# Combining a differential head's two probability maps before the transposes, and norming from the accumulators

## The chip, the cores and the metric

One core of a Trainium2 chip runs the whole program. The time is the device time of one execution in microseconds; the number quoted for a kernel is the median of its runs. The profiled execution is one further run, and its trace gives a span, from the first to the last instruction, and a start time for every instruction.

## What is computed

The program is two small transformer stacks run one after the other on 256 tokens of width 1024: four blocks (feed-forward, mixer, feed-forward) and then two larger layers. Every matrix is fp32. The mixer changes with the block. Block 2, and only block 2, uses the differential mixer, `mixer_c` of the reference:

```
q = q.reshape(B, nb, Q_BLOCK, HEADS_C, 2, HEAD_DIM_C).transpose(1, 0, 2, 3, 4, 5)    # 8 heads, 2 maps, 64
k = k.reshape(B, S, HEADS_C, 2, HEAD_DIM_C)
v = v.reshape(B, S, HEADS_C, 2 * HEAD_DIM_C)                                          # 128 wide, one for both maps
lam_full = jnp.exp(jnp.sum(lamf[0] * lamf[1])) - jnp.exp(jnp.sum(lamf[2] * lamf[3])) + lambda_init
...
    s = jnp.einsum('bqhmd,bkhmd->bmhqk', qblk, k).astype(jnp.float32) * scale + alibi
    s = jnp.where(allowed, s, NEG_INF)
    p = jax.nn.softmax(s, axis=-1)
    a = p[:, 0] - lam_full * p[:, 1]
    return jnp.einsum('bhqk,bkhe->bqhe', a.astype(v.dtype), v)
...
o = rms_norm(o, subln_g) * (1.0 - lambda_init)
return o.reshape(B, S, D) @ w_o
```

Each of the eight heads has two softmax maps over the same value rows; their difference, the second weighted by `lam_full`, is multiplied with the values, and each head's 128 outputs are normed by their own root mean square.

## The kernel before

The five engines run hand-written instruction streams that meet at semaphores. Outside attention the program is a chain of fp32 weight products on PE. Weights arrive in a ring of 9 slots and are split in two parts, by ACT (`high`) and DVE (`low`), up to three chunks ahead. The same stages run in the same order on each engine.

`units_of` lists what an attention has to do. For the differential mixer a unit is one map of one head for one tile of 128 queries: 16 units for tile t=0, which sees 128 keys, and 16 for tile t=1, which sees 256. `groups_of` joins units into groups: four units (two heads) in t=0, so groups 0 to 3, and two units (one head) in t=1, so groups 4 to 11. Either way a group has 512 score columns. An accumulator `acc` is one PSUM bank for two heads; in t=0 one group fills it, in t=1 two groups do. There are eight of them, named (t, b) here with b = 0 to 3.

All engines run a software pipeline over i, the number of the group, in their own function `attention`:

- PE in step i: scores of group i; transposes of group i-2 (it waits for `weighed`, the exponentials of ACT); the product of group i-3 with the values into the accumulator (it waits for the copy of the transposes out of PSUM). In step 13 the `tail` begins the transposes of the finished tile 0 of `o_rows` for the output product; their fourth pair comes after the loop, and its bank is the one that DVE frees with the first pair of `tile_low`.
- DVE in step i: scale and bias of the scores (L2000), the row maximum (L2002), for t=0 the copy of the transposes of group i-2 (L2010; ACT does it for t=1), and for a finished accumulator `evacuate`, here `f` of `differential`: reciprocal of four sums (L2064), the second map's factor times minus `lam_full` (L2066), the first map scaled (L2069), and the second added, a head at a time (L2071), into `o_rows`. The norm of the accumulator before is woven around it: `mean_of_heads` (L2046) ahead, `normed` (L2055) behind. In step 14 the `tail` is `tile_low`, the low part of the transposed tile 0 (L1941).
- ACT in step i: the sums of squares of a finished pair of heads (`head_squares`, L1432), for t=1 the copy of the transposes of group i-2 (L1295), and the exponentials of group i with their sums (L1457). After the loop come `head_squares` of (1, 2), `tile_high` of tile 0, and `head_squares` of (1, 3).
- POOL raises each mean to the power -0.5 (L1728), between `mean_of_heads` and `normed`.

Accumulators come from three banks in turn (`SUMMED`), score banks from three (`SCORES`), banks for transposes from two (`TB`). After attention PE goes on with the output product of tile 0, waits for tile 1's last norm, and never stops again for long in this block.

## Time and profile before

| | |
|---|---|
| median of 3 runs | 3040.71 us (3039.13 to 3049.1) |
| profiled execution | 3042.0 us, its span 3040.3 us |
| PE busy in the span | 2992.0 us, 98% |
| DVE, ACT, POOL busy | 1850.5, 1480.4, 84.1 us |
| mean granted TensorE clock | 0.999 of full speed |
| differential attention in the trace | from 1232.4 to 1268.4 us |

The trace's start times are counted from the start of the span. A row's duration is that of the instruction; the next instruction of an engine may start before it ends, so the distance between two starts is read beside it. "PE busy" counts pipelined matmuls to their modelled ends.

### The profile page before, as it was taken

To read this page: it belongs to the slowest core of one execution; us is meant where nothing else is said; L and a number is where in the kernel's file an instruction comes from. 1 tells how busy PE (TensorE), PEld (TensorE's weight loads), DVE (VectorE), ACT (ScalarE), POOL (GpSimd) and SP (SyncE) were. 2 spreads that over 40 slices of the span, in tenths; PEclk is the share of its full clock that TensorE was granted. 3 is DMA by queue.
4 is the path that set the end of the run, shared out by engine and by line. 5 is a ranking of instruction groups with operands and counts; after the bars stand their busy time and mean duration, and the time that the engine had idled before them with its cause. 6 is when DMAs were issued, how large, how long until landed. Compare 5 with 4: busy or idle time off the path is not lost.

```text
span 3040.3 us, 38290 instructions
## 1 busy us (share of the span) xinstructions
PE 2992.0 (98%) x15499; PEld 2526.9 (83%) x15499; DVE 1850.5 (61%) x2322; ACT 1480.4 (49%) x2163; POOL 84.1 (3%) x153
## 2 busy tenths in 40 slices
PE   8999999999999999999999999999999999999999
PEld 6889888888888888888888988897888889788887
DVE  5556655546655546755554665469775547977553
ACT  5445544435544435554443564354655434565542
POOL 0000000000000001000000000010000001000000
PEclk9999999999999999999999999999999999999999
DMA  7564455555555555265555635576244548615453
GB/s 229 186 208 141 161 192 177 194 190 199 183 181 190 190 181 186 84 201 188 193 180 175 219 119 193 179 203 210 84 159 150 190 166 226 200 69 171 152 189 126
DMA packets 302403, 532.98 MB, mean 175 GB/s; under 512 B 31074, under 2 KB 125204, under 8 KB 302228
## 3 DMA queue, kind: packets, MB, share of 16 engines
q1 hardware_dynamic: 288964, 511.63, 51.4%
q10 hardware_dynamic: 13264, 18.90, 1.8%
q8 instruction: 124, 2.03, 0.3%
q14 instruction: 51, 0.42, 0.0%
HBM read 528.33 MB, written 1.11 MB: 174 GB/s over the span
## 4 chain that ended last, share of the span: by engine, by line
PE 89%; DVE 8%; ACT 1%; issue 1%; DMA 1%; ACTq 0%; POOL 0%; SPq 0%; POOLq 0%; DVEq 0%
PE bank L724 85%; DVE sb_arena L2280 3%; DVE sb_parts L1819 2%; PE bank L1025 2%; PE bank L1053 1%; PE bank L805 1%; DMA sb_ring<-in_w_xq_dram 1%; ACT sb_parts L1321 0%; DVE sb_sc L2000 0%; PE bank L788 0%; PE bank L780 0%; ACT sb_sc L1457 0%; DVE sb_prT L2010 0%; POOL sb_rstd L1728 0%; DMA sb_ring<-in_ff_w_in_dram 0%
## 5 line engine op out<-in xcount | busy, mean ns | idle before, releaser
L1819 DVE TENSOR_TENSOR sb_parts<-sb_ring,sb_parts 128x2048 fp32r<-128x2048 f32 x480 | 1097.4, 2290 | 788.8 <-ACT sb_parts L1321 786.5
L724 PE MATMUL bank<-sb_parts,sb_hT_high 128*128 128x512 f32 (+1 forms) x4480 | 1370.0, 392 | 7.0 <-DVE sb_parts L1819 6.7
L1321 ACT ACTIVATE sb_parts<-sb_ring 128x2048 fp32r<-128x2048 f32 x480 | 914.5, 1913 | 790.6 <-PE bank L724 695.8
L724 PEld LDWEIGHTS bank<-sb_parts,sb_hT_high 128*128 128x128 f32 x4480 | 835.7, 188 | 184.4 <-DVE sb_parts L1819 11.0
L724 PE MATMUL bank<-sb_parts,sb_hT_low 128*128 128x512 f32 (+1 forms) x2240 | 853.0, 390 | 0.0
L724 PE MATMUL bank<-sb_parts,sb_hidden_high 128*128 128x512 f32 x1760 | 553.7, 395 | 0.0
L724 PEld LDWEIGHTS bank<-sb_parts,sb_hT_low 128*128 128x128 f32 x2240 | 420.9, 188 | 88.0
L724 PEld LDWEIGHTS bank<-sb_parts,sb_hidden_high 128*128 128x128 f32 x1760 | 328.3, 187 | 80.3 <-issue 0.6
L724 PE MATMUL bank<-sb_parts,sb_hidden_low 128*128 128x512 f32 x880 | 347.0, 394 | 0.0
L724 PE MATMUL bank<-sb_hT_high,sb_parts 128*128 128x256 f32 x1408 | 254.5, 283 | 0.0
L724 PEld LDWEIGHTS bank<-sb_hT_high,sb_parts 128*128 128x128 f32 x1408 | 220.1, 192 | 0.2
L724 PE MATMUL bank<-sb_hT_low,sb_parts 128*128 128x256 f32 x704 | 199.2, 283 | 0.0
L724 PEld LDWEIGHTS bank<-sb_parts,sb_hidden_low 128*128 128x128 f32 x880 | 164.7, 187 | 40.7
L724 PE MATMUL bank<-sb_parts,sb_oT_high 128*128 128x512 f32 (+1 forms) x616 | 177.9, 390 | 0.8 <-ACT sb_oT_high L1295 0.8
L1295 ACT ACTIVATE sb_hidden_high<-bank 128x512 fp32r<-128x512 f32 x110 | 60.4, 597 | 210.4 <-PE bank L1025 210.4
L1981 DVE TENSOR_TENSOR sb_hidden_low<-bank,sb_hidden_high 128x512 fp32r<-128x512 f32 x110 | 71.3, 686 | 107.4 <-ACT sb_hidden_high L1295 107.4
L724 PEld LDWEIGHTS bank<-sb_hT_low,sb_parts 128*128 128x128 f32 x704 | 135.1, 192 | 0.2
L724 PEld LDWEIGHTS bank<-sb_parts,sb_oT_high 128*128 128x128 f32 x616 | 112.6, 188 | 24.9 <-issue 3.0
L1457 ACT ACTIVATE sb_sc<-sb_sc,sb_nmax 128x256 f32<-128x256 f32 (+3 forms) x224 | 95.3, 427 | 73.7 <-DVE sb_nmax L2002 73.6
L1728 POOL TENSOR_TENSOR sb_rstd<-sb_mean_sq,sb_minus_half 128x1 f32<-128x1 f32 (+1 forms) x79 | 49.9, 632 | 2895.7 <-DVE sb_mean_sq L1838 2532.0
L1405 ACT ACTIVATE sb_prT<-bank,sb_rstd 128x512 f32<-128x512 f32 x100 | 69.2, 692 | 116.8 <-PE bank L724 116.8
L724 PE MATMUL bank<-sb_parts,sb_oT_low 128*128 128x512 f32 (+1 forms) x308 | 107.2, 386 | 0.0
(220 smaller groups left out, 2083.8 us busy)
## 6 DMA issues: line engine op xcount, KB each, us to landing
sb_ring<-in_ff_w_in_dram SPq DMA_DIRECT2D x160, 1024.0 KB, 5.2
sb_ring<-in_ff_w_out_dram SPq DMA_DIRECT2D x88, 1024.0 KB, 4.9
sb_ring<-in_w_gate_up_dram SPq DMA_DIRECT2D x40, 1024.0 KB, 5.2
sb_ring<-in_w_in_dram SPq DMA_DIRECT2D x38, 1024.0 KB, 5.2
sb_ring<-in_a_w_qkv_dram SPq DMA_DIRECT2D x24, 1024.0 KB, 5.3
sb_ring<-in_w_down_dram SPq DMA_DIRECT2D x22, 1024.0 KB, 5.0
sb_ring<-in_ff_w_in_dram SPq DMA_DIRECT2D x32, 512.0 KB, 4.8
sb_ring<-in_c_w_qkv_dram SPq DMA_DIRECT2D x12, 1024.0 KB, 5.1
```

The lines of the kernel that those rows point to most:

```text
L724: return nc.tensor.matmul(o, lhsT, rhs, start=start, stop=stop)
L805: ins = nc.tensor.transpose(o, i, ident[:, :])
L1025: ins = nc.tensor.transpose(bank[:, c * S + t * P:c * S + (t + 1) * P], hid_f[:, t, (2 * b + c) * P:(2 * b + c + 1) * P], ident[:, :])
L1053: ins = nc.tensor.transpose(bank[0:n, c:c + P], sc[:, (i - 2) % 3, k0:k0 + n], ident[:, :])
L1295: return nc.scalar.activation(o, i, ACT.Copy, scale=scale)
L1321: nc.scalar.activation(halves(n, slice(0, filled(n))).high, ring[:, raw_in[n], 0:filled(n)], ACT.Copy) \
L1405: nc.scalar.activation(silu[:, t, :], G.of((st, "gate", g, t))[:, :], ACT.Silu, scale=row_factor_of(st, t)) \
L1457: ins = nc.scalar.activation(part_of, part_of, ACT.Exp, bias=nmax[:, i % 3, j:j + 1], accum_out=sums[:, u["t"], u["col"]:u["col"] + 1])
L1728: pool.tensor_tensor(rstd[:, c0:c0 + n], mean_sq[:, c0:c0 + n], minus_half[:, 0:n], ALU.pow) \
L1819: V.tensor_tensor(both.low, ring[:, raw_in[n], 0:filled(n)], both.high.bitcast(F32), ALU.subtract) \
L1981: V.tensor_tensor(hidT.low[:, k:k + 2, :], G.of((st, "hid", g, b))[:, :].rearrange("p (c s) -> p c s", c=2), hidT.high[:, k:k + 2, :].bitc ...
L2280: ins = V.scalar_tensor_tensor(convT[:, c, :], src, wt, convT[:, c, :], ALU.mult, ALU.add)
```

## The change

Since both maps of a head meet the same value rows, the difference can be taken between the maps. The exponentials stay unnormalised: with first and second sums s1 and s2 the kernel now forms e1 - lam_full (s1/s2) e2, which is s1 times the wanted map. The factor s1 carries through to the output, and the norm removes it, if its guard EPS is multiplied by s1 squared.

The diff, with lines that are context left out:

```diff
@@ units_of
-                            acc=(st, "o", t, s // per), c0=(s % per) * width, width=width, col=s, head=s))
+                            acc=(st, "o", t, s // per), c0=(s % per if i % 3 == 0 else s // 2 % 2) * width,
+                            width=width, col=s, head=s))
@@ groups_of
+                maps = 2 if kind == "mix" and i % 3 == 2 else 1
-                                   rows=u["blocks"][0][1], blocks=len(u["blocks"]), width=P * n * len(u["blocks"]),
+                                   rows=u["blocks"][0][1], blocks=len(u["blocks"]), width=P * n // maps * len(u["blocks"]),
@@ PE attention
-                        pe.wait_ge(weighed.sem, weighed.at((st, i - 2)))
+                        if g["maps"] == 2:
+                            pe.wait_ge(dve_step.sem, dve_step.at((st, "combined", i - 2)))
+                        else:
+                            pe.wait_ge(weighed.sem, weighed.at((st, i - 2)))
-                        for j, u in enumerate(g["units"]):
+                        for j, u in enumerate(g["units"][::g["maps"]]):
...
@@ ACT head_squares
-                act.wait_ge(dve_read.sem, dve_read.at(acc))
+                act.wait_ge(matmul_done.sem, matmul_done.at((st, "pv", b if t == 0 else 5 + 2 * b)))
-                    ins = nc.scalar.activation(xn[:, 0, 512:640], o_rows[:, t, c:c + P], ACT.Square,
+                    ins = nc.scalar.activation(xn[:, 0, 512:640], G.of(acc)[:, m * P:(m + 1) * P], ACT.Square,
@@ ACT attention
-                    if differential and i >= 5 and groups[i - 5]["last"]:
-                        head_squares(st, groups[i - 5]["acc"])
+                    if differential and i >= 4 and groups[i - 4]["last"]:
+                        head_squares(st, groups[i - 4]["acc"])
@@ DVE
+            def combine(st, i, g):
+                t, c = g["t"], g["units"][0]["col"]
+                ratio = inv[:, t, c + 1:c + g["n"]:2]
+                dve.wait_ge(weighed.sem, weighed.at((st, i)))
+                step(V.reciprocal(ratio, sums[:, t, c + 1:c + g["n"]:2]))
+                step(V.scalar_tensor_tensor(ratio, ratio, lam[:, 6:7], sums[:, t, c:c + g["n"]:2], ALU.mult, ALU.mult))
+                for m in range(0, g["n"], 2):
+                    first, second = (sc[:, i % 3, n * g["kn"]:(n + 1) * g["kn"]] for n in (m, m + 1))
+                    ins = V.scalar_tensor_tensor(first, second, inv[:, t, c + m + 1:c + m + 2], first, ALU.mult, ALU.add)
+                ins.then_inc(dve_step.sem, dve_step.next((st, "combined", i)))
@@ DVE attention
+                    if means:
+                        means()
...
+                    if 1 <= i <= len(groups) and groups[i - 1]["maps"] == 2:
+                        combine(st, i - 1, groups[i - 1])
...
+                    if norms:
+                        norms()
@@ differential: mean_of_heads
+                    step(V.scalar_tensor_tensor(guard, first_sums, EPS / factor ** 2, first_sums, ALU.mult, ALU.mult))
                     dve.wait_ge(squared.sem, squared.at((st, "subln", t, b)))
-                    V.tensor_scalar(mean_sq[:, 8 * t + 2 * b:8 * t + 2 * b + 2], ssum[:, 2 * b:2 * b + 2], 1.0 / (P * factor ** 2),
-                                    EPS / factor ** 2, ALU.mult, ALU.add) \
+                    V.scalar_tensor_tensor(mean_sq[:, 8 * t + 2 * b:8 * t + 2 * b + 2], ssum[:, 2 * b:2 * b + 2],
+                                           1.0 / (P * factor ** 2), guard, ALU.mult, ALU.add) \
@@ differential: normed
-                        o = o_rows[:, t, h * P:(h + 1) * P]
-                        ins = V.scalar_tensor_tensor(o, o, rstd[:, 8 * t + h:8 * t + h + 1], subln[:, :], ALU.mult, ALU.mult)
+                        ins = V.scalar_tensor_tensor(o_rows[:, t, h * P:(h + 1) * P], G.of(acc)[:, m * P:(m + 1) * P],
+                                                     rstd[:, 8 * t + h:8 * t + h + 1], subln[:, :], ALU.mult, ALU.mult)
+                    settle(dve, ins, dve_read, acc)
@@ differential: f
-                    cols = inv[:, t, 4 * b:4 * b + 4]
-                    step(V.reciprocal(cols, sums[:, t, 4 * b:4 * b + 4]))
-                    step(V.tensor_scalar(cols[:, 1:4:2], cols[:, 1:4:2], lam[:, 6:7], None, ALU.mult))
-                    both = bank[:, :].rearrange("p (h m d) -> p h m d", h=2, m=2)
-                    t0 = tmp[:, 0:256].rearrange("p (h d) -> p h d", h=2)
-                    step(V.tensor_tensor(t0, both[:, :, 0, :], spread(cols[:, 0:4:2], P), ALU.mult))
-                    for h in range(2):
-                        ins = V.scalar_tensor_tensor(o_rows[:, t, (2 * b + h) * P:(2 * b + h + 1) * P], both[:, h, 1, :],
-                                                     cols[:, 2 * h + 1:2 * h + 2], t0[:, h, :], ALU.mult, ALU.add)
-                    ins.then_inc(dve_read.sem, dve_read.next(acc))
```

What is left of `f` waits for the accumulator and marks it open; `means` and `norms` of the next step then do its mean and norm. Only the last accumulator is finished at once.

Three places show how the instructions move. On DVE, one step of t=1 that finishes an accumulator, before: mean of the accumulator before, evacuation, norm, and then the scores of the next group (`sb_sc<-bank,sb_arena` is scale and bias, `sb_nmax` the maximum).

```order
L2046 TENSOR_SCALAR sb_mean_sq<-sb_ssum 128x2 [waits squared,matmul_done]
L2064 RECIPROCAL sb_inv<-sb_sums 128x4
L2066 TENSOR_SCALAR sb_inv<-sb_inv,sb_lam 128x2 [waits dve_step]
L2069 TENSOR_TENSOR sb_tmp<-bank,sb_inv 128x256 [waits dve_step]
L2071 SCALAR_TENSOR_TENSOR sb_o_rows<-bank,sb_inv,sb_tmp 128x128 [waits dve_step]
L2071 SCALAR_TENSOR_TENSOR sb_o_rows<-bank,sb_inv,sb_tmp 128x128
L2055 SCALAR_TENSOR_TENSOR sb_o_rows<-sb_o_rows,sb_rstd,sb_subln 128x128 [waits rstd_ready]
L2055 SCALAR_TENSOR_TENSOR sb_o_rows<-sb_o_rows,sb_rstd,sb_subln 128x128
L2000 SCALAR_TENSOR_TENSOR sb_sc<-bank,sb_arena 128x512 [waits transposed,scored]
L2002 TENSOR_REDUCE sb_nmax<-sb_sc 128x2 [waits dve_read]
```

The same place of the changed kernel, one whole step: the guard and the mean come first, then the scores, then the combination of the group before (`sb_sc<-sb_sc,sb_inv`), then the norm, which now reads a bank.

```order
L2069 SCALAR_TENSOR_TENSOR sb_inv<-sb_sums 128x2 [waits matmul_done,dve_read]
L2071 SCALAR_TENSOR_TENSOR sb_mean_sq<-sb_ssum,sb_inv 128x2 [waits squared,dve_step]
L2018 SCALAR_TENSOR_TENSOR sb_sc<-bank,sb_arena 128x512 [waits transposed,scored]
L2020 TENSOR_REDUCE sb_nmax<-sb_sc 128x2 [waits dve_read]
L1994 RECIPROCAL sb_inv<-sb_sums 128x1 [waits weighed]
L1995 SCALAR_TENSOR_TENSOR sb_inv<-sb_inv,sb_lam,sb_sums 128x1 [waits dve_step]
L1998 SCALAR_TENSOR_TENSOR sb_sc<-sb_sc,sb_inv 128x256 [waits dve_step]
L2081 SCALAR_TENSOR_TENSOR sb_o_rows<-bank,sb_rstd,sb_subln 128x128 [waits rstd_ready]
L2081 SCALAR_TENSOR_TENSOR sb_o_rows<-bank,sb_rstd,sb_subln 128x128
```

The five evacuation instructions per accumulator are gone, and three for every group have come. At the end of DVE's loop, before, nothing stood between the norm of the accumulator before and `tile_low` (`sb_oT_low`); in the changed kernel the guard, mean and norm of (1, 2) stand there:

```order
L1994 RECIPROCAL sb_inv<-sb_sums 128x1 [waits weighed]
L1995 SCALAR_TENSOR_TENSOR sb_inv<-sb_inv,sb_lam,sb_sums 128x1 [waits dve_step]
L1998 SCALAR_TENSOR_TENSOR sb_sc<-sb_sc,sb_inv 128x256 [waits dve_step]
L2081 SCALAR_TENSOR_TENSOR sb_o_rows<-bank,sb_rstd,sb_subln 128x128 [waits rstd_ready]
L2081 SCALAR_TENSOR_TENSOR sb_o_rows<-bank,sb_rstd,sb_subln 128x128
L2069 SCALAR_TENSOR_TENSOR sb_inv<-sb_sums 128x2 [waits matmul_done,dve_read]
L2071 SCALAR_TENSOR_TENSOR sb_mean_sq<-sb_ssum,sb_inv 128x2 [waits squared,dve_step]
L2081 SCALAR_TENSOR_TENSOR sb_o_rows<-bank,sb_rstd,sb_subln 128x128 [waits rstd_ready]
L2081 SCALAR_TENSOR_TENSOR sb_o_rows<-bank,sb_rstd,sb_subln 128x128
L1945 TENSOR_TENSOR sb_oT_low<-bank,sb_oT_high 128x128 [waits act_step,dve_read]
```

So two rounds of `normed` now precede `tile_low` where one did. On ACT, the end of the loop of the changed kernel has a pair of squares on either side of the copy of the last group:

```order
L1436 ACTIVATE sb_xn,sb_ssum<-bank 128x128 [waits squared,matmul_done]
L1436 ACTIVATE sb_xn,sb_ssum<-bank 128x128 [waits squared]
L1300 ACTIVATE sb_prT<-bank 128x256 [waits matmul_done,transposed]
L1436 ACTIVATE sb_xn,sb_ssum<-bank 128x128 [waits squared,matmul_done]
L1436 ACTIVATE sb_xn,sb_ssum<-bank 128x128 [waits squared]
L1300 ACTIVATE sb_oT_high<-bank 128x128 [waits transposed]
```

The pair after the copy is the old call behind the loop, `head_squares(st, (st, "o", NT - 1, 2))`, which the diff leaves in place. Step 13 of the loop now squares (1, 2) too, so this accumulator is squared twice, and DVE's mean waits for the second time. POOL's and SP's instructions are the same in both kernels.

## Rows read from the trace of the kernel before

**Rows 1.** The page: busy time of each engine, its share and instructions.
```profile
PE 2992.0 (98%) x15499; PEld 2526.9 (83%) x15499; DVE 1850.5 (61%) x2322; ACT 1480.4 (49%) x2163; POOL 84.1 (3%) x153
```

**Rows 2.** Windows: stretch, length, busy PE, PEld, DVE, ACT, POOL, PEclk, DMA.
```profile
1246.00:1254.00 8.00, 6.46 (x43) 5.69 (x44) 7.62 (x26) 5.38 (x22) 2.10 (x3) 1.00 0.01 3
```

**Rows 3.** The chain that ended last, 1205 to 1290: start, us, what.
```profile
1236.72 0.66 PE bank L1053 x4
...
1267.56 0.50 DVE sb_oT_low L1941 x2
...
1268.60 5.55 PE bank L724 x24
```

**Rows 4.** Timeline of DVE in the attention: start, us, instruction.
```profile
1233.50 0.76 DVE L2000 SCALAR_TENSOR_TENSOR sb_sc<-bank,sb_arena 128x256 f32<-128x256 f32 x2 [0.47 <-PE bank L724]
...
1234.90 0.75 DVE L2000 SCALAR_TENSOR_TENSOR sb_sc<-bank,sb_arena 128x256 f32<-128x256 f32 x2
...
1249.45 0.17 DVE L2064 RECIPROCAL sb_inv<-sb_sums 128x4 f32<-128x4 f32 x1
1249.66 0.23 DVE L2066 TENSOR_SCALAR sb_inv<-sb_inv,sb_lam 128x2 f32<-128x2 f32 x1
...
1250.91 0.61 DVE L2055 SCALAR_TENSOR_TENSOR sb_o_rows<-sb_o_rows,sb_rstd,sb_subln 128x128 f32<-128x128 f32 x2
1251.43 0.69 DVE L2000 SCALAR_TENSOR_TENSOR sb_sc<-bank,sb_arena 128x512 f32<-128x512 f32 x1
...
1252.75 0.16 DVE L2046 TENSOR_SCALAR sb_mean_sq<-sb_ssum 128x2 f32<-128x2 f32 x1
...
1260.81 0.68 DVE L2000 SCALAR_TENSOR_TENSOR sb_sc<-bank,sb_arena 128x512 f32<-128x512 f32 x1
```

**Rows 5.** Groups by form on DVE, 1233 to 1275: count, busy, mean ns.
```profile
L2071 DVE SCALAR_TENSOR_TENSOR sb_o_rows<-bank,sb_inv,sb_tmp 128x128 f32<-128x128 f32 x16 | 4.9, 347 | 0.3
L2055 DVE SCALAR_TENSOR_TENSOR sb_o_rows<-sb_o_rows,sb_rstd,sb_subln 128x128 f32<-128x128 f32 x16 | 4.9, 345 | 0.8 <-POOL sb_rstd L1728 0.8
...
L2000 DVE SCALAR_TENSOR_TENSOR sb_sc<-bank,sb_arena 128x256 f32<-128x256 f32 x8 | 3.0, 418 | 0.5 <-PE bank L724 0.5
...
L2010 DVE COPY sb_prT<-bank 128x512 f32<-128x512 f32 x4 | 2.7, 682 | 0.0
```

**Rows 6.** Single lines elsewhere: duration ns min/median/max, first and last start, forms.
```profile
L1887 DVE SCALAR_TENSOR_TENSOR sb_x<-sb_xn,sb_rstd,sb_x x48: 741/747/753, 203.3 to 1985.0; 128x512 f32<-128x512 f32 x48
...
L2188 DVE COPY sb_arena<-bank x12: 424/425/426, 261.7 to 1740.0; 128x256 f32<-128x256 f32 x12
```

**Rows 7.** Groups by form on ACT, 1233 to 1275.
```profile
L1457 ACT ACTIVATE sb_sc<-sb_sc,sb_nmax 128x256 f32<-128x256 f32 x16 | 8.0, 500 | 3.3 <-DVE sb_nmax L2002 3.3
```

**Rows 8.** Timelines late in the attention: ACT, PE and DVE.
```profile
1266.36 0.31 ACT L1432 ACTIVATE sb_xn<-sb_o_rows 128x128 f32<-128x128 f32 x1 [0.78 <-DVE sb_o_rows L2071]
...
1267.10 1.09 ACT L1295 ACTIVATE sb_oT_high<-bank 128x128 fp32r<-128x128 f32 x6
...
1257.69 0.60 PE L1053 MATMUL bank<-sb_ident,sb_sc 128*128 128x128 f32 x4
...
1259.02 1.03 PE L724 MATMUL bank<-sb_arena 128*128 128x256 f32 x4
1259.89 0.60 PE L1053 MATMUL bank<-sb_ident,sb_sc 128*128 128x128 f32 x4
...
1268.43 1.17 PE L724 MATMUL bank<-sb_parts,sb_oT_high 128*128 128x512 f32 x4
...
1272.03 0.17 DVE L2046 TENSOR_SCALAR sb_mean_sq<-sb_ssum 128x2 f32<-128x2 f32 x1 [0.39 <-ACT sb_xn L1432]
1273.01 0.61 DVE L2055 SCALAR_TENSOR_TENSOR sb_o_rows<-sb_o_rows,sb_rstd,sb_subln 128x128 f32<-128x128 f32 x2 [0.81 <-POOL sb_rstd L1728]
```

**Rows 9.** Windows where the granted clock fell, in a later layer.
```profile
2667.00:2670.00 3.00, 1.51 (x9) 0.95 (x8) 2.54 (x11) 2.21 (x3) 0.00 (x0) 1.00 0.22 33
...
2673.00:2676.00 3.00, 3.00 (x9) 2.35 (x8) 1.13 (x6) 2.97 (x11) 0.00 (x0) 0.50 0.00 0
```

35 lines of the change are left out of this document (21 added, 14 removed).

## Prediction

> **What bounds the kernel now.** I read the page first. PE is busy for 2992.0 of 3040.3 us [rows 1], so a change can only show where PE is not, or where it moves PE's own work. The edit touches one stage of some forty, the differential attention from 1232.4 to 1268.4 us: 36 us in all. Were the whole stage free the kernel would gain 1.2%. A window inside it has PE at 6.46 and DVE at 7.62 of 8 us [rows 2]: here DVE is the tighter engine. The chain that ended last says the same: PE runs it as far as the first transposes of the stage, and it ends in DVE's low part of tile 0, the last pair of transposes and then 5.55 us of output product without a gap [rows 3]. So two numbers decide: when DVE comes to the scores of the last group (group 11, at 1260.81 us [rows 4]), and how long it takes from there until the output product starts (at 1268.43 us [rows 8], 7.62 us later).
>
> DVE's own timeline gives prices as distances between starts. A four-unit step costs 1.40 us for scores and maximum (1233.50 to 1234.90), a two-unit step 1.32 (1251.43 to 1252.75). An evacuation costs 1.46 (1249.45 to 1250.91), a norm 0.52 (1250.91 to 1251.43), a reciprocal that the next instruction waits for 0.21 (1249.45 to 1249.66) [rows 4]. Beside the busy times this yields a rule of thumb: the next instruction starts 0.08 us before the end of one that it doesn't wait for (0.61 against 0.52 for the norm), and 0.04 after the end of one that it does (0.17 against 0.21). With it a copy of 128x512 costs 0.60 and the mean 0.08 [rows 5, 4].
>
> As a check, before: four steps at 1.40, seven at 1.32 (groups 4 to 10), four copies 2.4, five evacuations 7.3, four norms 2.1 and four means 0.3 make 26.9 us. From 1233.50 to 1260.81 are 27.31 us. DVE has nearly no idle time there, so its instructions add up to its time.
>
> **The change part by part.** On PE each group has half its transposes and half its value products. From one group's transposes to the next group's PE takes 2.20 us (1257.69 to 1259.89), 0.87 of it the scores [rows 8]; the other 1.33 halve, which leaves 1.5 us a step. PE only has to stay ahead of DVE, so this is worth nothing on the path: the cover is DVE's work, and PE had 1.5 us of 8 free already [rows 2]. On ACT the copies shrink to 128x256, hidden likewise.
>
> On DVE, removed: five evacuations before 1260.81, 7.3 us, and half of each of four copies. A 128x256 copy is busy for 0.42 us [rows 6], so it costs 0.34 in place of 0.60, four times: 1.0 us. Old mean and norm go too, 2.4 us.
>
> Added, the combination. Reciprocal 0.21; the tiny product with a pointer scalar, nearest row the 0.23 us of L2066 [rows 4], 0.27 with its wait. The large operation reads SBUF twice. For 128x128 its row is 345 ns and its step 0.26; for 128x256 the trace has the same operation from PSUM at 418 ns [rows 5], and from SBUF I interpolate 480 ns between 345 for 128 and 747 for 512 columns [rows 5, 6]. I take a step of 0.40, with bounds 0.34 (418 less 0.08) and 0.60 (had it to be the price of a 512-column maximum). So a four-unit group costs 0.21 + 0.27 + 2 x 0.26 = 1.00 us, a two-unit group 0.88. Groups 0 to 3 and 4 to 9 come before the scores of group 11: 4.0 + 5.3 = 9.3 us.
>
> Added, the mean with guard and the norm that must settle: guard 0.16 + 0.04 = 0.20 (priced as L2046, the same width with a constant [rows 4]), mean 0.08, norm 0.26 + 0.38 = 0.64 since the next instruction waits for the bank's release. That is 0.92 us, and five of them (accumulators of t=0 and the first of t=1) come before: 4.6 us. One new wait: the combination of group 0 needs its exponentials, which end at about 1236.68, when PE's first transposes were released [rows 3]; DVE is there at 1236.30, so 0.4 us, against 0.3 us that DVE waited for scores elsewhere. Later groups have the exponentials in time: two of 500 ns [rows 7] against 1.32 + 0.88 us of DVE work between the maximum and the combination of one group.
>
> Sum to the scores of group 11: +9.3 + 4.6 + 0.1 - 7.3 - 1.0 - 2.4 = +3.3 us, so they start at about T = 1264.1. Bounds: two-unit combinations at 0.67 (reciprocal 0.17, product 0.16, large step 0.34) and four-unit ones at 0.85 take 1.9 us off; at 1.1 us each they add 1.4.
>
> **The end of the stage**, counted from T. The maximum is done at 1.45, exponentials 11 at 2.6, combination 11 at 3.5. PE, after the product of group 9 and the six early transposes of tile 0, does the transposes of group 11 by 4.2. ACT has squared accumulator (1, 2) by then; it copies group 11 by 4.6 and squares (1, 2) a second time, 0.74 us (1266.36 to 1267.10 [rows 8]), until 5.4. DVE's mean waits for this, and the norm starts 0.98 us after the mean, POOL's power lying between (1272.03 to 1273.01 [rows 8]): 6.35. The norm costs 0.64 and only then does the low part of tile 0 start, at 7.0. From there to the output product it was 0.87 us (1267.56 [rows 3] to 1268.43 [rows 8]). Total 7.9 us, where it was 7.62. So the shorter route to the squares is given back by the second squaring and by the round through POOL that now stands in front of the low part. ACT's high part starts at 5.4 and is not what is late. Tile 1's last norm: squares after ACT's high part at about 9.3, norm done by 11.0; PE needs it at 7.9 + 5.55 = 13.4. It is hidden.
>
> Together +3.3 + 0.3 = +3.6 us, bounds +1.5 and +5.5. The stage is followed by PE work without gaps, so the shift reaches the end. The profiled run was 3042.0 us with a span of 3040.3, and the median is 3040.71: I add the shift to the median, 3044.3 us.
>
> **A rule against the trace.** The norm now reads a PSUM bank in place of SBUF. In this trace the two kinds of operand cost the same for 128 columns: 347 and 345 ns [rows 5], so I charge nothing. The Trainium skill, "VectorE: DVE Perf Modes", section "The TRN2 errata", has a fixed cost of 58 cycles for a SBUF source and 120 for PSUM at 0.96 GHz, an estimate of 0.065 us more for each norm instruction. By it the ten before T would add 0.65 us and the sum would be +4.2 instead of +3.6; the measured rows decide.
>
> **The rivals.**
>
> *The change is a gain of DVE work, and the stage shrinks.* For it speaks that the last evacuation chain of 1.46 us leaves the end and that t=0 steps carry less. If DVE were not the bound, its added 9.3 us would vanish in idle time. Against it: the check sum above leaves under 0.5 us idle in 27. If it held, the end would be 1.46 us shorter and the middle the same: 3039.3 us. Chance 0.06.
>
> *The granted clock falls at the end of the stage.* After its last transposes at T+4.2 PE has, until T+7.9, only the products of groups 10 and 11, about 1.1 us. In this kernel one such thin stretch, 1.51 us busy of 3, was followed by a window at 0.50 of the granted clock, 1.2 in place of 2.4 GHz [rows 9]; 1.5 us were lost. Before, with 6.46 of 8 us busy, it stayed at 1.00 [rows 2]. Then the time is 3044.3 + 1.6 = 3045.9 us. Chance 0.35, inside the same band. The Trainium skill, "TensorE: Matmul & The Clock Gate", Part 1, calls the throttled clock the default that activity releases; the trace's one fall is in line with that.
>
> *The clock falls for the whole attention: the other side.* PE's 1.5 us per step become 3.1 at half clock, where DVE now takes 2.7 on average (1.32 + 0.88 + half of 0.92). PE is then the bound in all twelve steps: 12 x 0.4 = 5 us, and 1.6 at the end, on top of 3.6: 3051 us, 0.33% slower. It decides only if the clock is low through nearly all steps. Against it: by these numbers PE still works 1.5 of 2.7 us in the middle, and more by the measure of the windows, which counts matmuls to their ends, no less than in the stretch before the fall. Chance 0.04.
>
> *Nothing moves.* If DVE's instructions had cover that I don't see, or the combination met its lower bound and the second squaring were early, the time is 3041 to 3042. Chance 0.10, and it can't be told from my forecast by the clock on the wall.
>
> The forecast without a clock fall has 0.45.
>
> **How the numbers follow.** A measurement of this kernel can tell about 0.3%, 9.1 us, from no change: that is 3031.6 to 3049.8. The forecast, its bounds of +1.5 to +5.5, the clock's 1.6 us, and the shrinking stage all lie inside it. Only the rival on the other side lies out, and the scatter of the runs shown, where one of three is 8.4 us above the median. So faster 0.01, within 0.3% 0.94, slower 0.05. The range runs from the shrinking stage, 3039.3, to the upper bound with the clock, 3047.8, and 2 us more for the scatter of a median.
>
> **What the profile would show.** Scores of the last group 3.3 us later than before, counted from the scores of the first; DVE busy in the middle with almost no idle time. Combination rows near 0.48 us for 128x256. Nine pairs of squares on ACT, the eighth right before the high part. DVE idle for nearly a microsecond ahead of the norm of (1, 2), waiting for POOL, with the low part behind it; the output product 34.9 + 3.6 us after the first scores. A clock below 1.00 around the end would show the second rival. I am wrong if DVE waits in the middle, for exponentials or for scores behind PE's products; if the large combination costs 0.6 us or more; or if PE's start doesn't hang on the low part of tile 0.

## The result, and the profile after

| | before | changed |
|---|---|---|
| median of 17 runs each | 3040.84 us | 3047.91 us |
| ratio | | 1.0021, interval 1.0014 to 1.0028 |
| profiled execution, its span | 3042.0, 3040.3 us | 3044.74, 3043.0 us |

The change costs 7.1 us by the medians and 6.4 us by the ratio (4.3 to 8.5). The prediction was 3044.3 us, range 3039.3 to 3049.8, with 0.94 on "within 0.3%". The measured median is inside the range and 3.6 us above the point. The stage's trace has a place for 1.6 us of that gap, and the rest stays open. Three runs at 4571.8 us (e4), 5339.5 us (e10) and 13122.9 us (before, beside e9 to e11) are in a slow state and stand in no mean, median or ratio below.

Two distances tell the stage: from the first scores on DVE to the last (group 11), and from the first scores to the output product on PE. Before they were 27.31 and 34.93 us [rows 4, 8]. After they are 30.67 and 38.41. The page of the changed kernel:

```profile
span 3043.0 us, 38167 instructions
...
PE 2986.1 (98%) x15427; PEld 2519.0 (83%) x15427; DVE 1850.1 (61%) x2330; ACT 1477.9 (49%) x2167; POOL 83.5 (3%) x153
```

DVE's total hardly moved (1850.5 before [rows 1]). PE has 72 matmuls less and is not faster for it. The timeline of DVE, changed kernel (start, us, instruction), shows the first scores, the first combination, one whole combination with the norm and the mean behind it, the last scores and the end:

```profile
1232.42 0.76 DVE L2018 SCALAR_TENSOR_TENSOR sb_sc<-bank,sb_arena 128x256 f32<-128x256 f32 x2 [0.47 <-PE bank L726]
...
1235.61 0.17 DVE L1994 RECIPROCAL sb_inv<-sb_sums 128x2 f32<-128x2 f32 x1 [0.33 <-ACT sb_sc L1461]
1235.81 0.22 DVE L1995 SCALAR_TENSOR_TENSOR sb_inv<-sb_inv,sb_lam,sb_sums 128x2 f32<-128x2 f32 x1
1236.07 0.61 DVE L1998 SCALAR_TENSOR_TENSOR sb_sc<-sb_sc,sb_inv 128x128 f32<-128x128 f32 x2
1236.60 0.75 DVE L2018 SCALAR_TENSOR_TENSOR sb_sc<-bank,sb_arena 128x256 f32<-128x256 f32 x2
...
1249.99 0.15 DVE L1994 RECIPROCAL sb_inv<-sb_sums 128x1 f32<-128x1 f32 x1
1250.18 0.22 DVE L1995 SCALAR_TENSOR_TENSOR sb_inv<-sb_inv,sb_lam,sb_sums 128x1 f32<-128x1 f32 x1
1250.43 0.48 DVE L1998 SCALAR_TENSOR_TENSOR sb_sc<-sb_sc,sb_inv 128x256 f32<-128x256 f32 x1
1250.84 0.60 DVE L2081 SCALAR_TENSOR_TENSOR sb_o_rows<-bank,sb_rstd,sb_subln 128x128 f32<-128x128 f32 x2
1251.47 0.16 DVE L2069 SCALAR_TENSOR_TENSOR sb_inv<-sb_sums 128x2 f32<-128x2 f32 x1
1251.67 0.16 DVE L2071 SCALAR_TENSOR_TENSOR sb_mean_sq<-sb_ssum,sb_inv 128x2 f32<-128x2 f32 x1
1251.75 0.69 DVE L2018 SCALAR_TENSOR_TENSOR sb_sc<-bank,sb_arena 128x512 f32<-128x512 f32 x1
...
1263.09 0.69 DVE L2018 SCALAR_TENSOR_TENSOR sb_sc<-bank,sb_arena 128x512 f32<-128x512 f32 x1
...
1268.35 0.16 DVE L2071 SCALAR_TENSOR_TENSOR sb_mean_sq<-sb_ssum,sb_inv 128x2 f32<-128x2 f32 x1 [1.03 <-ACT sb_xn L1436]
1269.32 0.61 DVE L2081 SCALAR_TENSOR_TENSOR sb_o_rows<-bank,sb_rstd,sb_subln 128x128 f32<-128x128 f32 x2 [0.81 <-POOL sb_rstd L1732]
1269.96 1.28 DVE L1945 TENSOR_TENSOR sb_oT_low<-bank,sb_oT_high 128x128 fp32r<-128x128 f32 x6
```

The reader sees the whole price here. A four-unit combination takes 0.99 us (1235.61 to 1236.60), a two-unit one 0.85 (1249.99 to 1250.84), norm, guard and mean together 0.91 (1250.84 to 1251.75). Nothing waits in between, so the new work adds straight to the stage. Up to the last scores the timeline notes only three waits of DVE behind its first instruction: the 0.33 us shown, 0.27 and 0.22. At the end DVE waits twice, for ACT's second squaring (1.03) and for POOL (0.81), before the low part may start at 1269.96.

PE's timeline in the changed kernel has the other half of the story:

```profile
1236.74 0.52 PE L1058 MATMUL bank<-sb_ident,sb_sc 128*128 128x128 f32 x2 [2.57 <-DVE sb_sc L1998]
...
1265.40 0.44 PE L1058 MATMUL bank<-sb_ident,sb_sc 128*128 128x128 f32 x2 [1.93 <-DVE sb_sc L1998]
...
1270.60 0.41 PE L790 MATMUL bank<-sb_ident,sb_o_rows 128*128 128x128 f32 x2 [2.25 <-DVE sb_oT_low L1945]
1270.83 1.82 PE L726 MATMUL bank<-sb_parts,sb_oT_high 128*128 128x512 f32 x4
```

It waits 2.57 us for the first combination and 2.25 us for the low part. The first four matmuls of the output product then take 1.82 us, where the same four took 1.17 [rows 8]. The windows of the changed kernel (stretch, length, busy PE, PEld, DVE, ACT, POOL, PEclk, DMA) say why:

```profile
1235.00:1238.00 3.00, 1.26 (x7) 1.26 (x8) 2.56 (x9) 2.12 (x12) 0.00 (x0) 0.83 0.40 142
1238.00:1241.00 3.00, 2.88 (x14) 2.42 (x14) 2.86 (x11) 1.85 (x9) 0.00 (x0) 0.61 0.00 0
1246.00:1254.00 8.00, 4.43 (x22) 2.65 (x21) 7.31 (x24) 4.78 (x21) 1.39 (x2) 1.00 0.00 1
1271.00:1274.00 3.00, 3.00 (x9) 2.35 (x8) 1.57 (x8) 2.88 (x7) 0.70 (x1) 0.51 0.01 3
1274.00:1277.00 3.00, 3.00 (x13) 2.40 (x13) 0.00 (x0) 0.00 (x0) 0.00 (x0) 0.92 0.00 0
```

The granted clock fell to its lower level, 1.2 GHz, twice in this stage, each time behind one of PE's long waits. The first fall is hidden in this execution: PE's few matmuls run while DVE sets the pace (2.86 of 3 us busy). The second lies on the path, in the chain of the changed kernel:

```profile
1271.01 7.16 PE bank L726 x24
```

The same 24 matmuls were 5.55 us before [rows 3]: 1.6 us lost. In the two profiled executions the changed kernel reaches its first scores 1.08 us earlier (1232.42 against 1233.50), loses 3.48 us up to the output product, and lies 4.27 us behind at the first transposes in the next feed-forward (1314.20 against 1309.93). Yet the spans differ by 2.7 us only. Here are the same transposes of a later layer in both kernels, before first, and a later wait of the changed kernel:

```profile
2669.69 0.88 PE L780 MATMUL bank<-sb_ident,sb_o_rows 128*128 128x128 f32 x6 [1.49 <-DVEq L1824]
...
2672.51 0.87 PE L782 MATMUL bank<-sb_ident,sb_o_rows 128*128 128x128 f32 x6 [1.18 <-DVEq L1828]
...
2798.47 1.72 PE L726 MATMUL bank<-sb_sc,sb_x 128*128 128x128 f32 x13 [1.48 <-DVE sb_arena L2423]
```

The distance is down to 2.82 us there, 1.5 us less, in work that the edit didn't touch. The fall that the execution of before had at 2673 [rows 9] comes after these rows, so it isn't what took them. It brings the distance down to 1.2 us for a while, but at 2798.47 the changed kernel waits 1.48 us where before does not, and in the end 2.7 us are left. So a shift of this stage does not reach the end whole. Why it shrinks was not tested.

### The profile page after: what moved, and what is told of

Its sections match the earlier page's. It is cut to its first block, busy times and chain, and to the rows that moved or that the text cites. A ratio compares the mean times of both kernels' runs of the same rounds, so it can differ in the third digit from the quotient of the medians.

```text
span 3043.0 us, 38167 instructions
## 1 busy us (share of the span) xinstructions
PE 2986.1 (98%) x15427; PEld 2519.0 (83%) x15427; DVE 1850.1 (61%) x2330; ACT 1477.9 (49%) x2167; POOL 83.5 (3%) x153
## 4 chain that ended last, share of the span: by engine, by line
PE 86%; DVE 8%; DMA 1%; ACT 1%; issue 1%; POOL 0%; ACTq 0%; SPq 0%; POOLq 0%; DVEq 0%
PE bank L726 83%; DVE sb_arena L2304 3%; DVE sb_parts L1823 2%; PE bank L1027 2%; PE bank L1058 1%; ACT sb_parts L1326 1%; PE bank L807 1%; DMA sb_ring<-in_w_xq_dram 1%; DMA sb_ring<-in_ff_w_in_dram 1%; DVE sb_sc L2018 0%; PE bank L790 0%; POOL sb_rstd L1732 0%; DVE sb_nmax L2020 0%; PE bank L782 0%; ACTq L1560 0%
```

## The experiments

All kernels are variants of the changed one. "Mean" is the mean time of the runs less that of the kernel before on the same chip, with its standard error. The clock is the mean over the runs, this kernel and then before. Distances are from one profile each. e1 to e4 share a chip, e5 to e8 another and e9 to e11 a third; e12 ran on a fourth.

| kernel | last scores | output product | against before | clock | mean | ratio [95%] |
|---|---|---|---|---|---|---|
| changed | 30.67 | 38.41 | +3.5 | 0.9971 | +6.2 ± 1.1 | 1.0021 [1.0014, 1.0028] |
| e5 changed again | 30.64 | 38.38 | +3.5 | 0.9971, 0.9984 | +4.9 ± 0.9 | 1.0018 [1.0008, 1.0027] |
| e1 one squaring | 31.15 | 37.90 | +3.0 | 0.9972, 0.9986 | +3.1 ± 0.7 | 1.0011 [1.0003, 1.0020] |
| e2 low part first | 30.66 | 37.28 | +2.4 | 0.9976, 0.9986 | +3.4 ± 0.7 | 1.0012 [1.0003, 1.0020] |
| e3 PE filled | 30.97 | 39.61 | +4.7 | 0.9982, 0.9986 | +4.3 ± 0.8 | 1.0015 [1.0006, 1.0024] |
| e4 first tile only | 26.25 | 33.87 | -1.1 | 0.9976, 0.9986 | -1.0 ± 1.2 | 0.9998 [0.9989, 1.0007] |
| e6 e1 and e2 | 31.13 | 37.11 | +2.2 | 0.9970, 0.9984 | +2.5 ± 0.9 | 1.0010 [1.0002, 1.0019] |
| e7 no combination | 21.38 | 28.36 | -6.6 | 0.9975, 0.9984 | -4.2 ± 1.0 | 0.9988 [0.9980, 0.9997] |
| e8 e4, high part first | 25.75 | 32.57 | -2.4 | 0.9973, 0.9984 | -0.4 ± 1.1 | 1.0000 [0.9991, 1.0009] |
| e9 POOL combines | 31.81 | 40.29 | +5.4 | 0.9969, 0.9986 | +6.5 ± 0.9 | 1.0021 [1.0011, 1.0030] |
| e10 e6, PE filled | 32.35 | 38.63 | +3.7 | 0.9979, 0.9986 | +3.5 ± 1.1 | 1.0012 [1.0003, 1.0021] |
| e11 e8, PE filled | 27.45 | 34.27 | -0.7 | 0.9981, 0.9986 | -2.8 ± 1.2 | 0.9992 [0.9983, 1.0001] |
| e12 e11 again | 27.45 | 34.26 | -0.7 | 0.9988, 0.9988 | -3.3 ± 0.6 | 0.9988 [0.9979, 0.9997] |

(For e12 the clock of before is without one run of 3045.57 us that shows 0.948; its time is in the mean.)

**The end of the stage.** In e1 the old squaring is taken out; in e2 the low part of tile 0 stands ahead of the guard, mean and norm of (1, 2).

```diff
@@ ACT, behind the loop (e1)
-                if i % 3 == 2:
-                    head_squares(st, (st, "o", NT - 1, 2))
@@ DVE attention, ahead of means() (e2)
+                    if tail and norms and i == len(groups) + 2:
+                        tail()
...
-                    if tail and i == len(groups) + 2:
+                    if tail and not norms and i == len(groups) + 2:
                         tail()
```

> The changed kernel without the second squaring of accumulator (1, 2). In the changed kernel the mean of (1, 2) starts at 1268.35 us, right after the second pair of squares; the guard was ready at 1267.35 and the first pair of squares at 1267.1. If the end of the stage hangs on the second squaring, the distance from the first scores to the output product falls from 38.4 to 37.4 us and the median by about 1 us. If it hangs on something else there (the copy of group 11, the transposes), the distance stays within 0.3 us of 38.4. The granted clock is not touched by this: theory 'thin PE stretches let the clock fall' expects a mean clock of 0.995 to 0.998 and a scatter of some 9 us between runs, as in the changed kernel.

> The changed kernel with DVE's low part of tile 0 moved ahead of guard, mean and norm of (1, 2) in step 14; the second squaring stays. If the round through POOL in front of the low part is what costs, the low part starts when ACT's first high pair is there, about 1268.5 in place of 1269.96, and the distance from first scores to output product falls from 38.4 to about 36.9 us. If PE's start hangs on ACT's high part or on the products of group 11, it falls by less than 0.5 us. Tile 1's last norm gets later by some 1.5 us, but PE needs it 5.6 us after its start, so no new wait is expected. The clock as in the changed kernel, a little better since the gap of PE at the end is shorter.

From the last scores to the output product the changed kernel takes 7.74 us, e1 6.75 and e2 6.62: 1.0 and 1.1 us less. In e1 the mean no longer waits for ACT, and POOL alone is left (DVE):

```profile
1268.70 0.16 DVE L2069 SCALAR_TENSOR_TENSOR sb_mean_sq<-sb_ssum,sb_inv 128x2 f32<-128x2 f32 x1
1269.67 0.61 DVE L2079 SCALAR_TENSOR_TENSOR sb_o_rows<-bank,sb_rstd,sb_subln 128x128 f32<-128x128 f32 x2 [0.81 <-POOL sb_rstd L1730]
```

In e2 the low part waits for ACT's high part, which stands behind the second squaring, so its stage is 37.28 us long and not the 36.9 expected:

```profile
1270.26 1.28 DVE L1945 TENSOR_TENSOR sb_oT_low<-bank,sb_oT_high 128x128 fp32r<-128x128 f32 x6 [1.58 <-ACT sb_oT_high L1300]
```

So both new pieces at the end are real. Each edit alone leaves a wait: e1 the round through POOL, e2 the high part behind the second squaring. The stage as a whole shrank by less than was expected of e1 (37.4 us, 37.90 measured). Its last scores come 0.5 us later than in the changed kernel, though the edit touches nothing ahead of them. The granted clock tells why: it is 0.88 and 0.55 in the two stretches from 1238 to 1244, so e1's first fall lies later in the stage, and DVE has to wait for the scores of group 4:

```profile
1243.33 0.69 DVE L2016 SCALAR_TENSOR_TENSOR sb_sc<-bank,sb_arena 128x512 f32<-128x512 f32 x1 [0.39 <-PE bank L726]
```

The same wait stands in the profiles of e4 and e6, and in those of the changed kernel, e5, e2 and e8 it does not. The clock of e1 fell once more behind PE's wait of 1.93 us for the combination of group 10:

```profile
1268.00:1271.00 3.00, 3.00 (x15) 2.76 (x15) 2.09 (x10) 1.81 (x10) 0.70 (x1) 0.50 0.02 5
1271.00:1274.00 3.00, 3.00 (x15) 2.51 (x16) 1.72 (x9) 2.56 (x7) 0.69 (x1) 1.00 0.01 3
```

There it met transposes and the last value products, while DVE and POOL were still on their way to the low part, and the output product ran at 5.50 us. The same kind of fall costs 1.6 us, 0.5 us or little, by where it lands.

e6 is both edits together.

> The changed kernel with one squaring of (1, 2) and with the low part of tile 0 ahead of guard, mean and norm of (1, 2). Each alone took 1.0 to 1.1 us off the end (7.74 us from the last scores to the output product became 6.75 and 6.62). If they are two waits in a row, both together give about 5.7 us; if PE's last products or the copy of group 11 are the next thing, about 6.2. The last scores stay 30.7 us after the first, so the stage is 36.4 to 36.9 us, still 1.5 to 2 us longer than before: DVE's added work is not touched. Mean time 2 to 3 us above before.

The end takes 5.98 us, 1.76 less than in the changed kernel. The expectation was 5.7 us for two waits in a row and 6.2 if something else came next; the low part now waits 0.93 us for ACT's high part. The output product still starts 2.2 us later than before, because 3.8 us of the middle stay, about 0.5 of them from the first fall, which is twice as long here as in the changed kernel (0.72, 0.50 and 0.64 from 1238 to 1247).

**The middle.** In e7 nothing is combined, so the second map is left out of the result, and PE waits for the exponentials alone.

```diff
@@ PE attention
-                            pe.wait_ge(dve_step.sem, dve_step.at((st, "combined", i - 2)))
@@ DVE attention
-                    if 1 <= i <= len(groups) and groups[i - 1]["maps"] == 2:
-                        combine(st, i - 1, groups[i - 1])
```

> The changed kernel without the combination: the second map is left out, so the result is only the first map's. This takes 4 x 1.00 and 6 x 0.87 us of DVE's work, 9.2 us, and one wait of 0.3 us out of the stretch from the first scores to the last. If DVE is the bound all the way, the last scores come 30.7 - 9.5 = 21.2 us after the first. If ACT or PE is close behind DVE, they come at 23 us or later. The thin stretches of PE get shorter, so the clock should fall less often than in the changed kernel.

The last scores come 21.38 us after the first, 9.3 less than in the changed kernel. That is the 9.3 us that the prediction charged, now measured by taking the work away. (The combinations alone are 4 x 0.99 + 6 x 0.85 = 9.1 us; waits of DVE change a little as well.) The granted clock stays up at the stage's start, where e7's PE has no wait for a combination and its first wait is 1.47 us:

```profile
1238.00:1244.00 6.00, 5.12 (x33) 4.07 (x32) 5.53 (x15) 5.91 (x31) 0.74 (x2) 1.00 0.00 0
```

At its end PE waits as long for the low part as in the changed kernel, and there is no fall: the granted clock is 1.00 from 1259 to 1283, and the first four matmuls of the output product take 1.15 us.

```profile
1260.73 0.41 PE L790 MATMUL bank<-sb_ident,sb_o_rows 128*128 128x128 f32 x2 [2.25 <-DVE sb_oT_low L1943]
```

So a wait of 2.25 us alone does not bring the fall. One caution: this profile is of the fastest of e7's twelve runs (3033.61 us, where their median is 3040.0), and their mean clock, 0.9975, lies below that of before. Other executions of e7 had falls that this profile doesn't show.

e4 combines in tile 0 alone; tile 1 keeps the old evacuation and the norm of `o_rows`.

```diff
@@ groups_of
-                maps = 2 if kind == "mix" and i % 3 == 2 else 1
+                maps = 2 if kind == "mix" and i % 3 == 2 and u["t"] == 0 else 1
@@ differential: f
+                    if t == 0:
+                        open_heads.append((t, b))
+                        return
...
+                    step(V.tensor_tensor(t0, both[:, :, 0, :], spread(cols[:, 0:4:2], P), ALU.mult))
```

> Maps combined before the transposes and the norm from the accumulators for tile 0 only; tile 1 is done as before. By DVE's prices tile 0 gains: a group costs 1.00 for the combination, 0.34 for the copy and 0.92 for mean and norm, where it cost 0.60 for the copy, 1.46 for the evacuation and 0.60 for mean and norm. Four groups: 9.0 against 10.6 us, so the distance from first scores to output product is 33.4 where it was 34.9 us before, and the end of the stage is that of before. Median 3039.5 if the clock stays, faster than before by too little to tell. Theory clock: PE is thin in tile 0 only, so at most one fall near the start, hidden by DVE. Rival: combining is a loss in either tile; then the distance is above 34.9.

The last scores come at 26.25 us: 1.1 earlier than before, 4.4 earlier than in the changed kernel. The rows explain it. In tile 0 an accumulator is one group, so one combination of 0.98 us replaces 1.46 of evacuation, and a DVE copy shrinks as well. In tile 1 an accumulator is two groups of 256 keys, so two combinations at 0.85 replace the same 1.46, and the copy that shrinks is ACT's. Most of the 4.4 us come from where the work stands in the pipeline. A group is combined one step after its scores, an accumulator is evacuated four steps after those of its last group. So up to the last scores tile 1 has six combinations and one more round of guard, mean and norm, where it had one evacuation: 6 x 0.85 + 0.91 - 1.46 = 4.6 us. The change gains in one tile and loses in the other.

In e8 ACT's high part of tile 0 also goes ahead of the squares of (1, 2).

```diff
@@ ACT, behind the loop
-                if i % 3 == 2:
-                    head_squares(st, (st, "o", NT - 1, 2))
                 tile_high((st, "oT"), 0, lambda kt: 1.0, oT)
                 if i % 3 == 2:
+                    head_squares(st, (st, "o", NT - 1, 2))
                     head_squares(st, (st, "o", NT - 1, 3))
```

> Combining in tile 0 only, and in addition ACT's high part of tile 0 ahead of the squares of (1, 2). In before the low part waits 0.71 us for the high part, which waits for those squares. The end should shrink from 7.62 to about 6.9 us, and the stage to 33.2 us where it was 34.9 us before. Tile 1's last norm is not later, since DVE comes to the mean of (1, 2) only after the low part. Mean time 1.7 us under before; a rival is that the freed time reappears ahead of tile 1's transposes, then the time is that of combining in tile 0 only.

The output product starts at 32.57 us, 2.4 us less than before and 1.3 less than in e4. The edit explains 0.8 of these (the end is 6.82 us long, 7.62 in e4). The other 0.5 stand ahead of the last scores: e8's first fall is half as long as e4's, and DVE has no wait for group 4. So tile 0 gains 1.1 to 1.6 us, and tile 1 loses 4.4 to 4.9, by how long that fall is. The chain of e8 ends in PE's own products now, with the last pair of transposes right behind them:

```profile
1264.24 2.02 PE bank L726 x16
...
1266.39 0.41 PE bank L790 x2
1266.80 5.55 PE bank L726 x24
```

But the mean time is that of before. The stage's gain is not seen in the time of the runs, and e8's mean clock is 0.9973 against 0.9984.

**The clock.** e5 is the changed kernel once more, with a profile of its own.

> The changed kernel itself once more, on the same chip as the next three, so that they can be compared with it. From first scores to output product 38.4 us unless the clock falls inside the attention; last scores 30.7 us after the first. Theory clock: more of its runs than of before's have a mean clock under 0.999, and its mean time lies 5 to 6 us above before's, 3.5 of it from the stage.

Its stage agrees to 0.03 us, it has the same two falls in the stage, and one at 2673 in a later layer. The first of the two stands in every profile whose PE waits 2.57 us or more for the first combination (the changed kernel and all of e1 to e12 but e7), and in neither of the two where that wait is about 1.5 us (before and e7). e3 issues the transposes and value products of each group twice into the same banks, so that PE has as much to do as before. PE's first wait stays at 2.57 us.

```diff
@@ PE attention, transposes and value products
-                        for j, u in enumerate(g["units"][::g["maps"]]):
+                        for j, u in (x for _ in range(g["maps"]) for x in enumerate(g["units"][::g["maps"]])):
```

> The changed kernel, but PE does every transpose and every value product of the differential attention twice, so that it has as much work there as before; results are the same. Theory clock: the changed kernel's median lies 7 us above before, of which DVE's work and the end of the stage explain 3.5; the rest are falls of the granted clock that follow thin stretches of PE. Then padding brings the mean clock back to 0.998 to 0.999, narrows the scatter, leaves the distance of 38.4 us nearly as it is (up to 0.5 us more at the end, where products of groups 10 and 11 are on or near the path) and lowers the median to about 3044. Rival: the excess has another cause (the weight transfer that ACT waits for near 1282 us, or later stages); then the median stays near 3048 or rises.

Its windows at the end show no fall, though the first fall, from 1238 to 1241, is there as in the others:

```profile
1268.00:1274.00 6.00, 4.35 (x37) 4.11 (x36) 3.12 (x13) 3.30 (x18) 0.88 (x2) 1.00 0.00 0
1274.00:1280.00 6.00, 6.00 (x31) 4.89 (x30) 1.35 (x7) 3.13 (x11) 0.70 (x1) 1.00 0.01 4
```

The output product is back at 5.55 us and the mean clock at 0.9982. The doubled work lengthens the stage by 1.2 us, though, 0.9 of them at its end, so most of the 1.6 us that the fall had taken are spent again. The median, expected at about 3044, is 3046.97 us. e10 is e6 with groups 0 to 9 doubled and the last two not; e11 is e8 with the doubling, where it touches groups 0 to 3.

```diff
@@ PE attention, transposes (e10, e11; the value products alike, with i - 3)
-                        for j, u in enumerate(g["units"][::g["maps"]]):
+                        for j, u in (x for _ in range(g["maps"] if i - 2 < 10 else 1) for x in enumerate(g["units"][::g["maps"]])):
```

> Both edits at the end, and the transposes and value products of groups 0 to 9 issued twice into the same banks, so that PE works as much as before through the loop and no more at its end. Theory: the times of the changed kernels lie above what their stage costs because PE's clock falls more often in this stage; with PE filled the stage costs about +2.2 us against before (scores of the last group +3.6, end -1.6), and the mean time of the runs lies +2 to +3 us above before's with a mean clock of 0.998 or more. Rival: the added clock loss has nothing to do with how full PE is in the loop; then mean clock stays at 0.997 and the mean time at the +2.5 us of both edits without filling. The stage itself should show 31.1 and 37.1 to 37.6 us, with no fall inside it.

> The combination in tile 0 alone with the high part first on ACT, and the transposes and value products of groups 0 to 3 issued twice, so that PE works as much as before. The stage should stay at 25.8 us to the last scores and 32.6 us to the output product, 2.3 us less than before. Theory: with PE filled its mean clock returns to 0.998 or more, and the time is 2 to 3 us under before's in mean and median, about 3040.8 where before has 3043 on such a chip (ratio 0.9992). Rival: filling PE changes nothing, the mean time is that of before as without filling (ratio 1.0).

> The same kernel as the run before it (combination in tile 0 alone, high part first, PE filled in groups 0 to 3), on another occasion, to see if 2 to 3 us under before is repeatable where one interval reached 1.0001. Theory: its stage starts the output product 34.3 us after the first scores when the clock falls early in it and 32.6 when it doesn't, against 34.9 before; the mean clock is 0.998 or more; ratio 0.999 to 0.9995. Rival: the first time was scatter, the ratio is 1.0 or above and the mean clock 0.997 as without filling.

The mean clock rises with filling in every pair (0.9971 to 0.9982, 0.9970 to 0.9979, 0.9973 to 0.9981 and 0.9988). The two sides of a pair ran on different chips, and before's own clock differs there (0.9984 beside the unfilled ones, 0.9986 to 0.9988 beside the filled), so 0.0002 to 0.0004 of each rise is not the filling's. The time doesn't follow each time. e10's mean is no better than e6's (+3.5 against +2.5). In its profile the clock fell nevertheless behind the wait for the first combination, and the doubled work at the lower level was then slower than DVE (PE 3.00, DVE 1.38 of 3 us):

```profile
1241.00:1244.00 3.00, 2.72 (x13) 2.72 (x14) 2.90 (x10) 1.95 (x11) 0.00 (x0) 0.50 0.00 0
1244.00:1247.00 3.00, 3.00 (x12) 2.54 (x12) 1.38 (x3) 1.25 (x8) 0.00 (x0) 0.51 0.00 0
```

It cost 1.2 us of distance to the last scores against e6, whose fall is as long: DVE waits 1.59 us for the scores of group 4 where it waited 0.39. So the forecast for e10, a stage of 37.1 to 37.6 us with no fall inside, missed (38.63), and that for e11 too (27.45 and 34.27 for 25.8 and 32.6). e12's profile shows the same. e11 and e12 lie 1.2 us above e4, whose fall is as long, and 1.7 above e8:

```profile
1238.00:1241.00 3.00, 2.33 (x11) 2.18 (x11) 2.86 (x10) 1.95 (x11) 0.00 (x0) 0.50 0.00 0
1241.00:1244.00 3.00, 3.00 (x13) 2.53 (x11) 1.41 (x4) 1.79 (x11) 0.00 (x0) 0.50 0.00 0
```

In time e11 and e12 are the best version found: 3039.82 and 3038.71 us where before had 3043.47 and 3041.92 beside them, ratios 0.9992 and 0.9988. The second interval lies below 1 and the first just touches it. So a version that beats before exists, by about 0.1%, and it beats the changed kernel by more. That the filling is what takes e8's 1.0000 there is not shown: the intervals overlap, and in the profiles the filled kernel has the longer fall and the longer stage. How often it happens in the runs without a profile is not known.

**Another engine for the combination.** e9 is e6 with the large step on POOL, as a product and a sum for each head, while DVE keeps the two small ones.

```diff
@@ POOL
+                                step(pool.tensor_scalar(second, second, inv[:, t, c + m + 1:c + m + 2], None, ALU.mult))
+                                ins = pool.tensor_tensor(first, first, second, ALU.add)
@@ DVE combine
-                    ins = V.scalar_tensor_tensor(first, second, inv[:, t, c + m + 1:c + m + 2], first, ALU.mult, ALU.add)
```

> The end as with both edits (one squaring, low part first), and the large step of the combination moved from DVE to POOL, as a product and a sum for each head; DVE keeps the reciprocal and the tiny product. Theory: DVE's instructions add up to the time, so taking away 4 x 0.52 + 6 x 0.40 = 4.5 us of large steps brings the scores of the last group from 31.1 us after the first to about 26.5, and the output product starts at about 32.5 to 33. Rival: POOL and the longer route are the bound. POOL's powers take 0.70 us for two columns, so two dependent operations of 256 columns may well take over 2 us, more than the step of DVE (1.32 + 0.44 + half of 0.92 = 2.2 us); then PE's transposes come late in every step, the scores of the last group stay at 31 us or later, DVE shows idle time that POOL or PE ends, and PE is thin enough for its granted clock to fall in the middle.

The rival holds: the last scores come at 31.81 us. The groups by form on POOL in the stage of e9 (count, busy, mean ns, idle ahead):

```profile
L1782 POOL TENSOR_SCALAR sb_sc<-sb_sc,sb_inv 128x256 f32<-128x256 f32 x8 | 7.4, 928 | 3.9 <-DVE sb_inv L2079 2.2 <-DVE sb_inv L2006 1.7
L1783 POOL TENSOR_TENSOR sb_sc<-sb_sc 128x256 f32<-128x256 f32 x8 | 5.8, 724 | 0.7
```

POOL needs 0.93 + 0.72 us for what DVE does in 0.48, plus 0.73 for the power of every accumulator. PE waits for it 15.1 us in all, the longest wait 4.4, and the clock is at 0.50 from 1241 to 1244:

```profile
1241.00:1244.00 3.00, 3.00 (x15) 2.87 (x15) 1.50 (x4) 0.01 (x1) 1.48 (x3) 0.50 0.00 0
```

The stage is 3.2 us longer than that of e6.

## Why the prediction came out as it did

**What bounds the stage: right.** DVE has almost no idle time in the middle, and its instructions add up to the distance. The shift to the last scores was forecast as +3.3 us and is 30.67 - 27.31 = +3.4. This is a small difference of large terms and could have come out by luck. It didn't: e7 measures the largest term, the combination, at 9.3 us, as charged. By parts the large step was taken as 0.40 and is 0.41 (1250.43 to 1250.84), a two-unit combination 0.85 for 0.88, a four-unit one 0.99 for 1.00, mean and norm 0.91 for 0.92, the first wait 0.33 for 0.4. A slip in the bounds has no weight: combinations at 1.1 us each add 0.4 + 1.3 = 1.7 us, not 1.4, and the bounds of +1.5 and +5.5 don't follow exactly from the figures given for them.

**The rule against the trace: the rows were right.** Groups by form on DVE in the changed kernel:

```profile
L2081 DVE SCALAR_TENSOR_TENSOR sb_o_rows<-bank,sb_rstd,sb_subln 128x128 f32<-128x128 f32 x16 | 4.8, 345 | 1.6 <-POOL sb_rstd L1732 1.6
L1998 DVE SCALAR_TENSOR_TENSOR sb_sc<-sb_sc,sb_inv 128x256 f32<-128x256 f32 x8 | 3.9, 484 | 0.3
```

The norm from the bank takes 345 ns, as it did from SBUF [rows 5]. The Trainium skill, "VectorE: DVE Perf Modes", section "The TRN2 errata", would have it 0.065 us dearer, by the prediction's estimate from its table; this operation shows nothing of that. The interpolated 480 ns of the large step are 484.

**The end of the stage: right, to 0.2 us.** The forecast was 7.9 us with the second squaring, the round through POOL and the low part in this order; the trace has 7.74. Each step is where it was put: squares done 5.2 us after the last scores (forecast 5.4), norm at 6.23 (6.35), low part at 6.87 (7.0). e1 and e2 confirm both pieces.

**What was off: the clock, and the way to the end.** The forecast added nothing for the clock, and "the granted clock falls at the end of the stage" was a rival at 0.35, with 3045.9 us. Both profiles of the changed kernel show that fall. It costs 1.6 us in one (7.16 against 5.55) and 1.4 in the other (6.99), about the price of the rival. With it the stage explains 3.5 + 1.6 = +5.1 us. The falls seen in the stage also fit the mean clock. The windows of 1235 to 1241 lack 0.17 and 0.39 of 3 us each, those of 1271 to 1277 0.49 and 0.08; at half speed that is 3.4 and 3.4 us, which lowers the mean over 3043 us by 0.0011. The runs of before and of the changed kernel show means of 0.9984 and 0.9971 (e5). The Trainium skill, "TensorE: Matmul & The Clock Gate", Part 1, has the lower clock as what a lack of activity brings. Both falls here stand behind waits of over 2 us, in agreement; e7's wait of 2.25 us without a fall shows that one wait of that length doesn't decide it.

"The stage is followed by PE work without gaps, so the shift reaches the end" was wrong in part. Between 1314 and the transposes near 2670 the shift falls from 4.27 to 2.82 us, and in e5 from 4.54 to 2.49 (1314.47 and 2672.18). So the agreement of the stage's +5.1 us with e5's mean of +4.9 ± 0.9, and with the interval of the main ratio (4.3 to 8.5), is partly luck. If some 1.5 us of the stage's shift are lost on the way, as in the profiles, the main +6.4 has nearly 3 us without a place, and e5's mean 1 to 2.

The reason for giving the fall only 0.35 was that it is not certain after a gap. The profiles bear that out in part: e3 has none at the end behind a wait of 1.65 us and e7 none behind 2.25, while the changed kernel, with 2.25 us of waiting after a thin middle, had it in two of two. The prediction took its one case, 1.51 us busy of 3, from a later layer. The same trace of before has a stretch as thin at the start of the stage itself, with no fall in it or behind it:

```profile
1235.00:1238.00 3.00, 1.54 (x15) 1.35 (x13) 2.93 (x7) 2.98 (x15) 0.00 (x0) 1.00 0.74 248
```

The first fall, at 1235 to 1241, was not foreseen at all. It comes with the change: PE waits 2.57 us for the first combination, where before it waited 1.46 us for the exponentials, and all twelve profiles with at least that wait have a fall behind it.

**The other rivals.** "The clock falls for the whole attention" is wrong: from 1246 to 1254 it is 1.00 with PE busy 4.43 of 8 us. "A gain of DVE work" is wrong as a whole and half true as to place: e4 shows the gain in tile 0. "Nothing moves" is excluded by the intervals.

**What stays open.** Time and stage don't agree for all variants. e7's stage is 6.6 us shorter and its mean only 4.2 ± 1.0 us, e8's 2.4 us and 0.4 ± 1.1; e12 gains more (3.3 ± 0.6) than its profile shows. What later layers take up of a shift differs from profile to profile and was not followed. Falls of the clock elsewhere, as around 2150 us in e2, e4, e8 and e10, or around 2673 us in before and e5, are in some profiles and not in others, and one profile for each kernel can't tell how the runs without one were made up.

## What to carry to other kernels

Where work moves from one side of a product to the other, count how many instructions of the bounding engine each side needs per tile: here the same idea gains 1.1 to 1.6 us in the tile with one group per accumulator and loses 4.4 to 4.9 in the tile with two. Count them up to the point that the next engine waits for, since the pipeline may have held the old ones back until behind it. Halving PE's work is worth nothing while another engine sets the pace. Count a new wait of the matmul engine twice, once as time and once as a chance of running the next stretch at half speed, and look whether that stretch is on the path. And after a restructuring look at what stands last in each queue: two leftovers in the order of the end, a second squaring and a norm ahead of the low part, cost 1.8 us of the 3.5. Last, follow a stage's shift through the layers behind it before adding it to the time of the whole.
